# A hybrid decoder step on one core: the decode sequences' masked values formed by VectorE instead of GpSimd

## The reference

```python
def _trunk_layer(x, lp, st):
    rw_shift, rw_S, rg_conv, rg_h, gdn_conv, gdn_S, gla_S = st
    x = x + 0.5 * _swiglu(_rmsnorm(x, lp['norm_ffn1']), lp['ffn1_gate'], lp['ffn1_up'], lp['ffn1_down'])
    h = _rmsnorm(x, lp['norm_mix'])
    proj = (h @ lp['w_in']).astype(F32)
    p_rw, p_rg, p_gdn, p_gla = jnp.split(proj, IN_SPLITS, axis=-1)
    o_rw, rw_shift, rw_S = _rwkv7_group(p_rw, rw_shift, rw_S, lp)
    o_rg, rg_conv, rg_h = _rglru_group(p_rg, rg_conv, rg_h, lp)
    o_gdn, gdn_conv, gdn_S = _gdn_group(p_gdn, gdn_conv, gdn_S, lp)
    o_gla, gla_S = _gla_group(p_gla, gla_S, lp)
    mixed = jnp.concatenate([o_rw, o_rg, o_gdn, o_gla], axis=-1).astype(x.dtype)
    x = x + mixed @ lp['w_out']
    x = x + 0.5 * _swiglu(_rmsnorm(x, lp['norm_ffn2']), lp['ffn2_gate'], lp['ffn2_up'], lp['ffn2_down'])
    return x, (rw_shift, rw_S, rg_conv, rg_h, gdn_conv, gdn_S, gla_S)
```

## Time and profile before

| | us |
|---|---|
| median of 3 runs | 1412.89 |
| lowest and highest | 1412.67 and 1414.23 |
| the profiled execution | 1414.94 |
| its span, first to last instruction | 1413.1 |
| TensorE busy in the span | 1371.8 (97%) |
| VectorE busy | 862.5 (61%) |
| ScalarE busy | 681.4 (48%) |
| GpSimd busy | 87.7 (6%) |

### The profile page before, as it was taken

The page is one execution under the profiler, slowest core; times in us unless marked ns, Lnnn a source line. Parts: engine busy times, 40 slices in busy tenths (PEclk is TensorE's granted clock), DMA queues, the critical chain, the costliest instruction groups (busy, mean ns, idle before and its releaser), DMA issues. The chain is left out here.

```text
span 1413.1 us, 31528 instructions
## 1 busy us (share of the span) xinstructions
PE 1371.8 (97%) x12556; PEld 1327.0 (94%) x12556; DVE 862.5 (61%) x1302; ACT 681.4 (48%) x938; POOL 87.7 (6%) x116
## 2 busy tenths in 40 slices
PE   7999999999999999999999999999999899999997
PEld 6999999889988999999999999998898789999997
DVE  5655534897776756653475554359986667555433
ACT  6554433835345645443364543356454447545332
POOL 2000000100130200000010000010001302000000
PEclk9999999999999999999999999999999999999999
DMA  7544444323212554444454444433222035444451
GB/s 280 173 151 149 149 141 149 112 69 97 65 46 85 183 165 148 148 149 145 148 184 149 148 148 149 148 126 99 78 89 77 22 132 164 148 148 148 149 150 51
DMA packets 50766, 185.87 MB, mean 132 GB/s; under 512 B 5760, under 2 KB 6272, under 8 KB 50176
## 3 DMA queue, kind: packets, MB, share of 16 engines
q1 hardware_dynamic: 49104, 177.37, 39.3%
q10 hardware_dynamic: 1584, 7.35, 1.4%
HBM read 180.14 MB, written 4.56 MB: 131 GB/s over the span
## 5 line engine op out<-in xcount | busy, mean ns | idle before, releaser
L459 PE MATMUL ps<-xh,wh 128*128 128x320 f32 x1952 | 613.2, 314 | 13.9 <-DVE xl L1464 13.1
L1442 DVE TENSOR_TENSOR wl<-raw,wh 128x1024 fp32r<-128x1024 f32 x332 | 408.5, 1231 | 337.1 <-ACT wh L1085 336.5
L461 PE MATMUL ps<-xh,wl 128*128 128x320 f32 x1952 | 603.6, 309 | 0.0
L460 PE MATMUL ps<-xl,wh 128*128 128x320 f32 x1952 | 603.4, 309 | 0.0
L1085 ACT ACTIVATE wh<-raw 128x1024 fp32r<-128x1024 f32 x332 | 349.1, 1054 | 400.1 <-PE ps L461 395.3
L459 PEld LDWEIGHTS ps<-xh,wh 128*128 128x128 f32 x1952 | 366.8, 188 | 25.4 <-issue 9.1
L460 PEld LDWEIGHTS ps<-xl,wh 128*128 128x128 f32 x1952 | 367.1, 188 | 0.9
L461 PEld LDWEIGHTS ps<-xh,wl 128*128 128x128 f32 x1952 | 366.9, 188 | 0.0
L459 PE MATMUL ps<-hid_h,wh 128*128 (+1 forms) x704 | 217.9, 310 | 2.5 <-DVE hid_l L1486 2.5
L461 PE MATMUL ps<-hid_h,wl 128*128 (+1 forms) x704 | 217.5, 309 | 0.0
L460 PE MATMUL ps<-hid_l,wh 128*128 (+1 forms) x704 | 217.5, 309 | 0.0
(11 more groups left out here) (286 smaller groups left out, 998.4 us busy)
## 6 DMA issues: line engine op xcount, KB each, us to landing
raw<-wts SPq DMA_DIRECT2D x332, 512.0 KB, 3.5
ms<-mst ACTq DMA_DIRECT2D x2, 1440.0 KB, 7.0
mout<-ms ACTq DMA_DIRECT2D x2, 1440.0 KB, 6.6
x<-xT SPq DMA_DIRECT2D x4, 320.0 KB, 4.9
yT<-x SPq DMA_DIRECT2D x4, 320.0 KB, 2.2
cs<-cst SPq DMA_DIRECT2D x1, 652.0 KB, 8.2
pr<-par ACTq DMA_DIRECT2D x1, 429.0 KB, 5.7
pr<-par ACTq DMA_DIRECT2D x1, 425.0 KB, 5.2
```

Of the source, the lines that this page charges most:

```text
L459: pe.matmul(out, a, rh, start=start, stop=False)
L460: pe.matmul(out, a, rl, start=False, stop=False)
L461: return pe.matmul(out, b, rh, start=False, stop=stop)
L1442: tt(wl[:, s, :], raw_of(layer, n), wh[:, s, :].bitcast(F32), ALU.subtract).then_inc(lo_ready.sem, 1)
```

## The change

The function `masked` goes from GpSimd's program into VectorE's, and its four calls into the hand-written list of the rounds: `VM[0]` behind `gla_chain()`, `UM[0]` behind `g_r(1)`, `UM[1]` behind `rg_root(2)`, `VM[2]` behind `g_m(2)`. They are signalled in another order, so that TensorE's waits on `VM` count (2, 3, 4) in place of (3, 4, 2). The step counts of the two engines follow.

```diff
-V_STEPS, A_STEPS, G_STEPS = 93, 32, 14 + 3 * 6
+V_STEPS, A_STEPS, G_STEPS = 97, 32, 28
...
-                on(pe, layer, "VM", (3, 4, 2)[g])
+                on(pe, layer, "VM", (2, 3, 4)[g])
...
+                def masked(dst, src, made, name="seqh", n=DECB // 2):
+                    on(ve, layer, *made)
+                    sm = C(name).unsqueeze(2).broadcast_to([128, n, 64])
+                    for p in range(2):
+                        ins = tt(dst[p].rearrange("q (s v) -> q s v", s=n), src[:, DEC, p, :].unsqueeze(1).broadcast_to([128, n, 64]), sm, ALU.mult)
+                        say(ins, "VM") if p else st(ins)
...
                     gla_chain()
+                    masked(VM[0], rVt, ("rw_rows",))
 
                     g_r(1)
+                    masked(UM[0], UU[0], ("rU", 1))
                     rg_root(0)
                     rg_root(1)
                     g_u(1)
                     rg_root(2)
+                    masked(UM[1], UU[1], ("gU", 1))
                     rw_shift()
                     centering()
                     g_m(1)
...
                     g_m(2)
+                    masked(VM[2], lVt, ("v_rows",), "seqm", DECB)
                     rg_scan()
...
-                on(gp, layer, in_read)
-                masked(VM[0], rVt)
-                on(gp, layer, "v_rows")
-                masked(VM[2], lVt, "seqm", DECB)
-                on(gp, layer, "rU", 1)
-                masked(UM[0], UU[0])
-                on(gp, layer, "gU", 1)
-                masked(UM[1], UU[1])
```

More of the change, by code:

```diff
@@ L2171, in decay @@
                         say(gp.tensor_tensor(v, v, d_, ALU.mult), "dec_decay")
[L2173 to L2178, removed]
-                decay(1)
-                on(gp, layer, in_read)
-                masked(VM[0], rVt)
-                on(gp, layer, "v_rows")
-                masked(VM[2], lVt, "seqm", DECB)
-                on(gp, layer, "rU", 1)
-                masked(UM[0], UU[0])
-                on(gp, layer, "gU", 1)
-                masked(UM[1], UU[1])
+                decay(1)
                 decay(2)
```

## The result

| | before | changed |
|---|---|---|
| median of the timed runs | 1414.28 us (20 runs) | 1416.68 us (20 runs) |
| the profiled execution, its span | 1413.1 us | 1413.9 us |
| VectorE busy | 862.5 us | 869.5 us |
| GpSimd busy | 87.7 us | 77.1 us |

What follows compares the result with a forecast made beforehand. TensorE was taken to bound the kernel, with VectorE's list bounding round 1 of layer 1. Terms 0.89 + 0.44 = +1.33 us took the span from 1413.1 to 1414.4, the median to 1414.2; range 1413.5 to 1415.0, chance 0.40.

Steps and rivals of the forecast that it cites:

- The prices: VectorE's masks: 0.41 us each for small, 0.69 for larger instructions; a small pair 0.66 us of the list, at most 0.82.
- idle time behind `VM[2]`: Round 2 to the end, both layers: VectorE's idle 2.16 us at g_u(3) covers VM[2]'s up to 1.4 us; cost nothing.
- GpSimd's removed work: 16 instructions, 11.9 us busy, leave GpSimd; they ran beside the other engines, so removal is worth nothing.
- The code gap in `known(1)`: Layer 1, behind the wait at the store: TensorE's 0.58 us code gap should vanish and give back 0.58 us.
- In layer 1 the step: Layer 1, round 1: store 1.47 us later, less 0.58 us given back by the code gap, nets 0.89 us.
- The move of the store itself: Layer 1, round 1: the masks delay VectorE's state store by 0.15 + 0.66 + 0.66 = 1.47 us.
- The new wait of 0.5 us at `m_products(1)`: Layer 1, round 1: UM[0] delays g_u(1), so TensorE waits 0.57 us, taken out of the later store wait.
- Layer 2, round 1: VM[0] and UM[0] vanish in VectorE's idle 2.63 us; UM[1] costs 0.66 less 0.22 at the store, 0.44 us.
- Layer 2 falls better: Rival: layer 2's 2.4 us code gap or lowered clock may not recur; gap of 0.6 means -1.8 us, 1412.4; chance 0.10.
- The clock: Rival: in layer 1 the longer waits lower TensorE's clock, losing 1.7 us; +3.0 in all, 1415.9; chance 0.18.
- The shared port: Layer 1: decay(2) collision costs VectorE 0.91 us, only its victim changing in the sum; rival that it goes: 1413.3, chance 0.06.

Runs made afterwards that it cites:

- e2: Changed kernel with VM[2] alone left on GpSimd, the three small masks on VectorE: 1416.47 us, ratio 1.0014 to the kernel before.
- e1: Changed kernel with only VM[2] formed by VectorE, the three small masks left on GpSimd: 1414.83 us, ratio 1.0002 to the kernel before.

## Why the forecast was right in kind and too small

**What held.** The place: the three small masks carry the loss (e2), the large one nothing (e1). The prices: 0.42 and 0.68 us, a pair 0.67 in the list, and VectorE busy 869.5 us for a forecast of about 870. `g_u(3)` still has idle time behind `VM[2]`, 0.96 us instead of 2.16 in layer 1. GpSimd's removed work gained nothing that shows. The code gap in `known(1)` is absent in both profiles of the changed kernel's layer 1, as forecast. But two of the four profiles of the kernel before do not have it either, so it is not shown that the change took it away. In layer 1 the step gave 0.89 us and the pair of profiles showed 0.89; that exactness is luck, since layer 1's rounds vary from 27.2 to 29.5 us among the profiles of the kernel before. The means over all profiles of the two kernels are 28.2 and 29.2. The move of the store itself was forecast well: counted from the start of the rounds it came 1.43 us later, for a forecast of 1.47. The new wait of 0.5 us at `m_products(1)` did not show in the first profile's layer 1, where a code gap of 0.52 us just ahead of it held TensorE up instead, but in layer 2 and in the repeat it did.

**The step that failed** is the one named "Layer 2, round 1", and with it the term of 0.44 us. It had two errors. It took `VM[0]` and `UM[0]` as covered by 2.63 us of VectorE's idle time, which hung on TensorE's code gap of 2.4 us, and took 0.22 off `UM[1]` for the idle time at the store. I wrote that gap into the program; it is the property of an execution. The kernel before has it in two of four profiles, the changed kernel in neither of its two, and two of its variants have one of 1.6 and 1.8 us. The second error is a reading: "TensorE had waited for this store already" rests on the 0.2 us of the earlier trace rows, and that wait stands in front of round 3. In front of round 2 TensorE did not wait, because behind the gap it had worked at a clock of 0.61.

What the runs showed in its place: without the gap layer 2 behaves like layer 1, with 2.6 us of waiting in front of round 2 against 1.3. The term is 1.3 us there, where I had 0.44. Added to layer 1's 0.89 it makes 2.2 us, and the measured difference of the means is 2.2 with a standard error of 0.4. This agreement proves less than it seems to. It takes both kernels without the gap, and half of the profiles of the kernel before have it; how often either kernel has it cannot be told from four and two profiles. And the clock, below, may hold a part of the same 2.2 us.

The rival "Layer 2 falls better" thought of the gap's absence as a gain of 1.8 us. Within the kernel before it is a gain of that size: the rounds of layer 2 took 31.0 and 30.7 us with the gap, 28.2 and 29.1 without. But the kernel before goes without it in half of its profiles too, so it is no gain of the change, and behind the gap lies VectorE's list, which the change had made longer: without the gap the changed kernel took 30.9 and 30.2 us.

**The clock.** The rival said that the clock would fall in layer 1 behind the longer wait. In neither profile of the changed kernel did it: from 421 to 426 us the granted clock was 1.00 in both. It falls at other places in the profiles of both kernels, in the first profile of the changed one around 1098 to 1106 us, ahead of the changed part. What the rival described did happen in layer 2: in the second profile the clock fell right behind the wait of 2.0 us, and that stretch lost about 1.7 us (an estimate, above). The kernel before, in the two profiles with the gap of 2.3 us, lost the clock behind the gap in the same way. The mean over the runs is lower by 0.0008 +- 0.0004, good for 0.6 us. So part of the loss may come that way; how often the longer waits cause it stays open. The Trainium skill, page "TensorE: Matmul & The Clock Gate", section "What's actually happening", says that the gate's window runs free of the kernel, so that the same kernel can meet it at another point each time; the scatter of the clock among identical runs (0.991 to 0.998 in the changed kernel) agrees, and so do the two profiles of the changed kernel, in one of which the clock fell behind the wait of 2.0 us and in the other it did not.

**The shared port.** I had charged nothing for a collision on the changed kernel's side. In layer 2 it appears there (1.23 us instead of 0.49), but it does in the kernel before as soon as the code gap is absent (1.40). The Trainium skill's rule of an exclusive lock, page "SBUF — State Buffer", section "SBUF: two separate sides", agrees with the fourth profile of the kernel before, where line 1776 ran through in its 0.49 us and the wait passed from one engine to the other:

```profile
414.24 1.41 POOL L2171 TENSOR_TENSOR ms<-ms,lnt 128x512 f32<-128x512 f32 x1 [2.60 <-PE ps L791]
...
414.24 0.49 DVE L1776 TENSOR_SCALAR ar<-ar 128x640 f32<-128x640 f32 x1
...
415.01 1.32 DVE L1779 SCALAR_TENSOR_TENSOR ar<-ar 128x640 f32<-128x640 f32 x1
```

`decay(2)`, 1.06 us elsewhere, lasted 1.41, ending at 415.65; line 1779, 0.82 elsewhere, lasted 1.32 and ended 0.7 us behind it.

## What to carry to other kernels

Idle time that comes from an engine waiting for nothing the program asks for ("issue") is no cover: before it is charged against an added cost, look whether the same stretch has it in the other layer or in another execution. And before a wait in a list is taken for the one in question, look in the timeline for where it stands: the 0.2 us that I built on belonged to the next round. When an engine has 38% of its time free, a step handed to it still costs its full length if it lands between two links of a recurrence; moved to a place where the engine waits for another anyway, the same instructions cost nothing that could be measured. And before moving work off a lightly loaded engine, look at what is left there: one remaining instruction of GpSimd that stood in VectorE's way was worth 1.4 us, more than all that the removed ones gave.

## What the runs showed of the hardware that I had not expected

- TensorE's stop for code goes by the arrival of the code, not by TensorE. In layer 1 it ended at 421.20 and 421.19 us in two kernels that reached it 1.2 us apart; the packet of code had started at 418.66 and 418.75. The six code gaps of 1.6 us and more in layer 2, each in another kernel or copy, ended 2.2 to 2.4 us after the start of the last packet of code.
- The gap in layer 2 goes with a transfer of weights just ahead of it. In the six profiles with a gap of 1.6 us or more, the 16 KB of code started 3.1 to 3.3 us after the 512 KB of weights had been issued (1105.60 and 1108.82 in the first profile). In nine of the eleven others it started before the issue or within 1.1 us of it (1106.20 and 1107.17 in the first profile of the changed kernel, 1108.68 and 1108.21 in the third of the kernel before). The last two lie between, with 2.7 and 2.9 us; one has a gap of 0.2 us there, the other none. That looks like code queued behind data. No experiment moved the transfer, so it is not shown.
- Identical kernels differ by up to 0.1% between sets of 12 runs, and each 0.001 of mean granted clock goes with 0.8 us.
